# The first network's second and third row pieces by seven block products for eight

## What is computed

```python
def _swiglu(h, w_up, w_down):
    gate, up = jnp.split(h @ w_up, 2, axis=-1)
    return (jax.nn.silu(gate) * up) @ w_down

def _layer(x, W, st, is_prompt, page_table, mem):
    x = x + 0.5 * _swiglu(_rms_norm(x, g[0]), W['ffa_up'], W['ffa_down'])
    p = _rms_norm(x, g[1]) @ W['w_in']
    ...
    x = x + jnp.concatenate([o_rw, o_ml, o_nsa], axis=-1) @ W['w_out']
    x = x + _mem_attend(_rms_norm(x, g[2]), st['mem_kv'], W['mem_w_q'], W['mem_qk_g'][0], W['mem_w_o'])
    x = x + 0.5 * _swiglu(_rms_norm(x, g[4]), W['ffb_up'], W['ffb_down'])
```

## Time and profile before

| | |
|---|---|
| median of 3 runs | 3776.53 us (3775.8 to 3785.59) |
| the profiled execution | 3781.91 us, its span 3780.2 us, mean granted TensorE clock 0.941 |
| TensorE busy | 3462.8 us (92% of the span) |
| VectorE / ScalarE / GpSimd busy | 1558.4 / 640.7 / 304.4 us |
| chain of work that ended last | 82% TensorE, 9% VectorE, 3% transfers |
| second network's products (line 4420) | 879.0 us, 5544 instructions |
| first network's products (lines 411 and 421) | 682.4 us, 2112 instructions, and 332.8 us, 1056 instructions |

### The profile page before, as it was taken

The page is one execution under the profiler, slowest core; times in us unless marked ns, Lnnn a source line. Parts: engine busy times, 40 slices in busy tenths (PEclk is TensorE's granted clock), DMA queues, the critical chain, the costliest instruction groups (busy, mean ns, idle before and its releaser), DMA issues.

```text
span 3780.2 us, 51473 instructions
## 1 busy us (share of the span) xinstructions
PE 3462.8 (92%) x20460; PEld 2568.7 (68%) x20460; DVE 1558.4 (41%) x3874; ACT 640.7 (17%) x1525; POOL 304.4 (8%) x396
## 2 busy tenths in 40 slices
PE   6999898999999999997886968888888999999998
PEld 4666565666567777675664734444577998899998
DVE  3444603323322323313643458744364555344333
ACT  1000011001010101012223326550112111211111
POOL 3111100000000000001001100000012340000000
PEclk8999999999999999998687879999999999999999
DMA  6565554232334332334337413022035675456775
GB/s 159 172 184 175 174 155 108 87 98 76 88 115 117 101 102 75 95 120 112 48 79 165 131 54 122 7 74 83 15 120 179 209 229 188 130 166 208 233 235 184
DMA packets 630137, 488.74 MB, mean 129 GB/s; under 512 B 95068, under 2 KB 590028, under 8 KB 625420
## 3 DMA queue, kind: packets, MB, share of 16 engines
q1 hardware_dynamic: 601820, 400.62, 36.2%
q0 software_dynamic: 13824, 67.12, 5.8%
q10 hardware_dynamic: 14256, 17.71, 1.3%
HBM read 419.85 MB, written 70.73 MB: 130 GB/s over the span
## 4 chain that ended last, share of the span: by engine, by line
PE 82%; DVE 9%; DMA 3%; issue 2%; SPq 2%; ACT 2%; DVEq 0%; POOL 0%; ACTq 0%; POOLq 0%
PE psum L4420 21%; PE psum L411 17%; PE psum L421 9%; PE psum L442 7%; PE psum L451 4%; PE psum L3745 3%; PE psum L1387 2%; DVE arena L3602 1%; PE psum L3511 1%; PE psum L3521 1%; PE psum L2683 1%; PE psum L3903 1%; PE psum L3500 1%; PE psum L4018 1%; PE psum L2724 1%
## 5 line engine op out<-in xcount | busy, mean ns | idle before, releaser
L4420 PE MATMUL psum<-arena 128*128 128x192 f32 (+1 forms) x5544 | 879.0, 320 | 22.9 <-POOL arena L4413 10.1
L4420 PEld LDWEIGHTS psum<-arena 128*128 128x128 f32 x5544 | 863.5, 192 | 39.2 <-issue 12.7
L411 PE MATMUL psum<-arena 128*128 128x384 f32 (+1 forms) x2112 | 682.4, 478 | 21.8 <-DVE arena L559 11.8
L411 PEld LDWEIGHTS psum<-arena 128*128 128x128 f32 x2112 | 398.1, 193 | 250.2 <-issue 22.8
L421 PE MATMUL psum<-arena 128*128 128x384 f32 (+1 forms) x1056 | 332.8, 472 | 0.0
L421 PEld LDWEIGHTS psum<-arena 128*128 128x128 f32 x1056 | 197.3, 190 | 113.0 <-issue 0.7
L442 PE MATMUL psum<-arena 128*128 128x384 f32 (+3 forms) x816 | 268.2, 484 | 6.0 <-DVE arena L559 6.0
L442 PEld LDWEIGHTS psum<-arena 128*128 128x128 f32 (+1 forms) x816 | 151.5, 190 | 100.8 <-issue 22.2
L4558 DVE SCALAR_TENSOR_TENSOR arena<-psum,arena 128x192 f32<-128x192 f32 (+1 forms) x336 | 113.4, 345 | 197.5 <-PE psum L4420 195.8
L451 PE MATMUL psum<-arena 128*128 128x264 f32 (+3 forms) x576 | 135.6, 397 | 0.0
L3745 PE MATMUL psum<-arena 128*128 128x384 f32 (+1 forms) x384 | 123.9, 480 | 6.1 <-issue 6.1
...
...
## 6 DMA issues: line engine op xcount, KB each, us to landing
arena<-in_ffa_up SPq DMA_DIRECT2D x132, 512.0 KB, 5.3
arena<-in_ffb_up SPq DMA_DIRECT2D x88, 512.0 KB, 4.3
...
```

The source lines that it names most:

```text
L411: ins = mm(b[:, 0:n], w[:, g, k], hC[:, k, 0:n], start=(k == 0), stop=(k == KD - 1))
L4420: ins = pe.eng.matmul(out, left[:, k], right[:, k], start=(first and k == 0), stop=(k == n - 1), skip_group_check=True)
```

## The change

Pieces 1 and 2 of the first network are computed as the second network is. The code of the second network becomes a set of functions for any `Net`, `NET_A` being pieces 1 and 2 of the first and `NET_B` the three pieces of the second; piece 0 of the first stays as it was. For `NET_A` the weight sums are not stored: GpSimd and VectorE make them in both pieces. The ring `wring` holds gate weights (2 slots), lift weights (3) and one slot of sums, at the places where the projection's slabs lie, so that the first loads of a piece wait for the projection's last slabs (`begins`), and the first slabs for the network's last products. The dense step now comes before the lane step for TensorE, VectorE and ScalarE, and GpSimd weaves its sums with its lane steps. In both networks VectorE's steps are cut at other points: the last product's evacuation and the third weight sum now stand after the `yield`. The first product of a group no longer waits for the weight sums. The core of the diff (the `Net` versions of `load_lift` and so on replace those of the second network, which are otherwise the same):

```diff
-        wring = arena.take(P, 3, SLAB)
+        wring = arena.take(P, 5 * D + 3 * 512)
...
+        hT_all = arena.take(P, 3 * KD // 2 * (PIECE // 2))
+        act_all = arena.take(P, FH * PIECE)
+        actT = act_all.rearrange("p (f c) -> p f c", f=FH)
...
+        KEPT = FT + len(PASSES) * KD // 2
+        HW = PIECE // 2
+        gate_w, lift_w = wring[:, 0:2 * D].rearrange("p (s x) -> p s x", s=2), wring[:, 2 * D:5 * D].rearrange("p (s x) -> p s x", s=3)
+        sums_w = [wring[:, 5 * D:5 * D + 3 * 512], arena.array[:, consts_at:consts_end]]
+        hB, hT = hC, hT_all.rearrange("p (t k c) -> p t k c", t=3, k=KD // 2)
+        actB = actT[:, 0:6]
...
+        def begins(net, m):
+            return not net.joined and m % KEPT < 3
+
+        def load_lift(sp, net, m):
+
+            kind, c, q, x = net.groups[m]
+            s, _, n0 = loads_of(net, m)
+            if begins(net, m):
+                proj_used(sp, c - 1, 11 if s == 2 else 10)
+                if m >= KEPT + 2:
+                    sp.wait_ge(products_made, net.products[m - 3, "last"])
+            elif m >= 3:
+                sp.wait_ge(products_made, net.products[m - 3, "last"])
+            if 3 <= m < net.made + 3:
+                wait_third_stored(sp, net, m - 3)
+            sp.wait_ge(slab_in[s], n0)
+            w, src = left_of(net, m), weights_of(net, m, 1)
+            n = pairs_of(net, m)
+            dst = lift_w[:, m % 3, 0:2 * n * P].rearrange("p (k c) -> p k c", k=2 * n)
+            if m >= net.made:
+                src, dst = src[:, n:2 * n] if kind == "up" else src[:, 1:2 * n:2], w["A22"]
+            sp.eng.dma_start(dst, src, allow_slow_non_contiguous=True).then_inc(slab_in[s], 16)
+
+        def load_gate(sp, net, m):
+
+            c, s = net.groups[m][1], loads_of(net, m)[0]
+            if begins(net, m) and m % KEPT < 2:
+                proj_used(sp, c - 1, 9)
+            elif m >= 2:
+                sp.wait_ge(products_made, net.products[m - 2, "P2"])
+            if 2 <= m < net.made + 2:
+                sp.wait_ge(weights_summed, net.weights_0 + m - 1)
+                sp.wait_ge(evacuated, net.evacuations[m - 2, "S3"])
+            n = pairs_of(net, m)
+            sp.eng.dma_start(gate_w[:, m % 2, 0:2 * n * P].rearrange("p (k c) -> p k c", k=2 * n), weights_of(net, m, 0),
+                             allow_slow_non_contiguous=True).then_inc(slab_in[s], 16)
+
...
+        def load_group(sp, net, m):
+            load_lift(sp, net, m)
+            load_gate(sp, net, m)
+            if m >= net.made:
+                load_sums(sp, net, m)
...
+        def load_item(sp, n):
+
+            c, r = divmod(n, ITEMS)
+            if c == 3:
+                return
+            s, _, n0 = LOADED["in", c, r]
+            if r < KEPT and c:
+                load_group(sp, NET_A, KEPT * (c - 1) + r)
+                return
+            if r < KEPT:
...
+        def weight_sums_gp(gp, net, m):
+
+            w = left_of(net, m)
+            wait_group(gp, net, m)
+            if m >= 2:
+                gp.wait_ge(products_made, net.products[m - 2, "P3"])
+                wait_sums_stored(gp, net, m - 2)
+            gp.eng.tensor_tensor(w["S1"], w["A21"], w["A22"], ALU.add).then_inc(gpsimd_done, 1)
+            gp.wait_ge(gpsimd_done, gp.done(gpsimd_done))
+            gp.eng.tensor_tensor(w["S2"], w["S1"], w["A11"], ALU.subtract).then_inc(gpsimd_done, 1)
+            gp.wait_ge(gpsimd_done, gp.done(gpsimd_done))
+            gp.eng.tensor_tensor(w["S4"], w["A12"], w["S2"], ALU.subtract).then_inc(weights_summed, 1)
+            gp.wait_ge(weights_summed, net.weights_0 + m + 1)
+
+        def net_gp(gp, net, c):
+            if net.joined:
+                gp.wait_ge(out_v[2], 9 + NB + 2 * KD)
+            else:
+                proj_used(gp, c - 1, 11)
+            weight_sums_gp(gp, net, chunk_of(net, c)[0])
+            for m in chunk_of(net, c):
+                if (m + 1) % KEPT:
+                    weight_sums_gp(gp, net, m + 1)
+                yield
+                if net.groups[m][0] == "up":
...
+        def last_pe(pe, net, m):
+
+            kind, c, _, _ = net.groups[m]
+            pe.wait_ge(evacuated, net.evacuations[m, "u2" if kind == "up" else "P7"])
+            pe.wait_ge(summed, net.h_sums(c, 4) if kind == "up" else net.act_sums(m, 4))
+            product(pe, x_bank(net, m), left_of(net, m)["A22"], right_of(net, m)["T4"], first=False)
+
+        def net_pe(pe, net, c):
+            for m in chunk_of(net, c):
+                A, B = left_of(net, m), right_of(net, m)
+                up = net.groups[m][0] == "up"
+                x, y, z = x_bank(net, m), y_bank(net, m), z_bank(net, m)
+                if m == chunk_of(net, c)[0]:
+                    pe.wait_ge(h_made, pe.due(h_made, KD) - 4)
+                if m % KEPT or net.joined and m:
+                    pe.wait_ge(evacuated, net.evacuations[m - 1, "g2" if net.groups[m - 1][0] == "up" else "P3"])
+                wait_group(pe, net, m)
+                product(pe, x, A["A11"], B["B11"])
+                if m < net.made:
+                    pe.wait_ge(weights_summed, net.weights_0 + m + 1)
+                pe.wait_ge(summed, net.h_sums(c, 1) if up else net.act_sums(m, 1))
+                product(pe, z, A["S1"], B["T1"])
+                yield
+                if net.pends(m - 1):
+                    last_pe(pe, net, m - 1)
+                if up:
+                    pe.wait_ge(copies_made, net.copied(m, 0))
+                    pe.wait_ge(summed, net.h_sums(c, 2))
+                else:
+                    pe.wait_ge(evacuated, net.evacuations[m, "P1"])
+                    pe.wait_ge(summed, net.act_sums(m, 2))
+                product(pe, x, A["S2"], B["T2"], first=False)
+                if net.pends(m - 1):
+                    pe.wait_ge(evacuated, net.evacuations[m - 1, "last"])
+                product(pe, y, A["A12"], B["B21"])
+                if up:
+                    pe.wait_ge(copies_made, net.copied(m, 1))
+                else:
+                    pe.wait_ge(evacuated, net.evacuations[m, "P5"])
+                product(pe, z, A["S4"], B["B22"], first=False)
+                if up:
+                    yield
+                    pe.wait_ge(copies_made, net.copied(m, 2))
+                else:
+                    pe.wait_ge(evacuated, net.evacuations[m, "P6"])
+                if m < net.made:
+                    pe.wait_ge(evacuated, net.evacuations[m, "S3"])
+                pe.wait_ge(summed, net.h_sums(c, 3) if up else net.act_sums(m, 3))
+                product(pe, x, A["S3"], B["T3"], first=False)
+                if not net.pends(m):
+                    last_pe(pe, net, m)
...
+        def last_dve(v, net, m):
+
+            kind, c, q, x = net.groups[m]
+            h, X = half_of(c), x_bank(net, m)
+            v.wait_ge(products_made, net.products[m, "last"])
+            if kind == "down":
+                to_x(v, net, m, "last", 1, 0, X)
+                if not net.joined and q == len(PASSES) - 1:
+                    v.wait_ge(evacuated, net.evacuations[m, "last"])
+                    for k in (2 * x, 2 * x + 1):
...
+        def net_dve(v, net, c):
...
+                    to_x(v, net, m, "P1", 0, 0, x)
+                    to_x(v, net, m, "P5", 1, 1, z)
+                    yield
+                    last_dve(v, net, m - 1)
+                    third_sum_dve(v, net, m)
+                    to_x(v, net, m, "P6", 0, 1, x)
...
+                yield
+                if net.pends(m - 1):
+                    last_dve(v, net, m - 1)
+                third_sum_dve(v, net, m)
+                v.wait_ge(products_made, net.products[m, "P2"])
+                v.wait_ge(copies_made, net.copied(m, 0))
+                e.tensor_tensor(s1, y, s1, ALU.add).then_inc(evacuated, 1)
...
+                yield
+                v.wait_ge(products_made, net.products[m, "P7"])
+                e.tensor_tensor(s5, x, s5, ALU.add).then_inc(evacuated, 1)
...
+        def scale_and_sum_dve(v, net, gi, c):
+
+            c0, n = CH[c]
+            scale_begin_dve(v, n)
+            for half in range(2):
+                for k in range(4 * half, 4 * half + 4):
+                    scale_one_dve(v, gi, k, xT[:, k, c0:c0 + n], hB[:, k, 0:n], n)
+                v.wait_ge(h_made, v.counts[h_made.name])
+                first_h_sum_dve(v, net, c) if half == 0 else other_h_sums_dve(v, net, c)
...
+        def dense_dve(v, c):
+            ahead = c < 2
+            if c:
+                v.wait_ge(proj_full, A_A * c)
+                scale_and_sum_dve(v, NET_A, 0, c)
+            for _ in net_dve(v, NET_A, c) if c else plain_dve(v):
...
-                for _ in alternate(3, lane(gp, p, rw_begin_gp, rw_make_gp, rw_chain_gp), lane(gp, p, ml_begin_gp, ml_make_gp, ml_chain_gp)):
+                lanes = lane(gp, p, rw_begin_gp, rw_make_gp, rw_chain_gp), lane(gp, p, ml_begin_gp, ml_make_gp, ml_chain_gp)
+                if p == 0:
```

(3 more changed lines are left out.)

855 lines of the change are left out of this document (390 added, 465 removed).

## The result

The changed kernel takes 3829.7 us (median of four runs, 3822.9 to 3836.4) where the kernel before takes 3778.3 beside it: 1.0133 times the time, 95% interval 1.0109 to 1.0156. It is slower by some 50 us; the prediction was 3741, faster. The profiled execution has a span of 3821.0 us, 40.8 more than that of before.

A forecast was written before the change was run, and what follows sets the result against it. TensorE was taken to bound the kernel, nearly without gaps. 105.5 - 24 - 4 - 40 - 5 + 3 = 35.5 us off the profiled 3781.9 gave 3746, or 3741 against the median of 3776.5; range 3703 to 3789.

The forecast's parts named there:

- the price of the products: Pieces 1 and 2: 1848 half-width products each at 162.5 and 135.8 ns, 105.5 us less if nothing waits.
- the price of GpSimd's disturbance: Middle of both pieces: lane operations with two SBUF inputs grow by a quarter, raising 12 us a piece to 17 and 23.
- the clock: TensorE at 1.2 GHz behind two long starts and clusters of short waits: 5 us lost (0 to 15).
- starts, ends and middle waits: Pieces 1 and 2: 24 us later starts, 4 us for squares at the ends, 40 us of waits in the middle.
- the lane step of lines 1664 to 1683: A VectorE lane step that now follows a down group: 2.8 us of TensorE waiting.
- the second network: First product no longer waits for GpSimd, VectorE's steps stand beside products they read: 3 us gained (5 lost to 8 gained).
- the forecast: The main case, chance 0.52: the whole kernel faster, 3712 to 3765 us.
- the rival of a blocked VectorE: GpSimd's sums hold up every lane operation and VectorE in turn holds up P2: 3796 us, slower, chance 0.17.
- the two start waits: Sign of being right: TensorE waits before the lanes' first matmuls, some 17 us in piece 1, 7 in piece 2.
- Waits on GpSimd's third sum: Sign of being wrong: TensorE waiting for that weight sum in the middle of a piece; no size given.
- the cover that holds: Rival: lane steps start early enough, middle waits 12 us and starts 20, 3706 us in all; chance 0.20.
- late weights: Rival: gate loads land late, piece 2's 22 up groups wait 1 to 2 us each, 3774 us; chance 0.11.

The follow-up runs named there:

- Alone against alone: Old and new kernel with each piece's recurrent lanes run after the next piece's dense work instead of woven in: piece 1 353.2 us old form, 329.5 new.
- the thin sums: Changed kernel with GpSimd's first-network weight sums, from the third group on, made over 2 of every 128 columns: 3759.5 us, 0.9934 of the kernel before.

## Why the prediction was wrong

In the two pieces together the kernel before takes 855.6 us and the changed one 918.1: 62.5 more, where the terms of the sum gave 32.5 less. The steps that failed are the price of the products (105.5 us less, "if nothing waits"), the price of GpSimd's disturbance (16 of the 40 us for the middle) and the clock (5 us). The miss of 95 us splits into:

- **The products: 74.5 us.** Forecast 105.5 less, measured 656.8 - 625.8 = 31.0 less. Two errors stand in this one term. I took the old form's price from stretches full of lanes and the new form's from the second network, which has few; "the form thus costs what its columns cost" compared unlike neighbours. Alone against alone the saving is 65.4 us, so 40 of the 74.5 are this. The other 34 are what the lanes cost the new form more than the old, and that is the clock. At the full-clock prices of 169.6 and 143.7 ns the new products would take 579.0 us; I put the 46.8 above that down to 1.2 GHz, an estimate from two windows. The old ones lost some 5 us in this way: line 411 takes 336.5 and 283.5 ns in the two windows below, where the clock was 1.00, and 339.1 and 288.0 over the pieces. The breaks between short runs cost the new form no more than the old. **The clock term of 5 us** held the idea and not its size.
- **Idle time of TensorE: 17.8 us.** It grew by 85.8 (60.2 + 53.7 against 19.7 + 8.5) where starts, ends and middle waits made 68. The first 82 and 66 us hold 35.4 us more idle time than before, where I had 24: the long waits came, but the first product of piece 1 waited 7.9 us instead of 4.8 (5.1 in the kernel with the sums on VectorE, whose four scalings take 2.21 us instead of 5.05), and short waits of 1.3 to 2.3 us followed. The ends hold 2 us less than before, not 4 more. In the middle I counted 40 and find 24 and 28. With the thin sums it is 22.7 in both middles together, where I had counted 12 a piece without disturbance: that sum came out right, though not place by place, as the lane step of lines 1664 to 1683 shows; what GpSimd adds did not, 30 us of middle waits instead of 16.
- **Lanes and squares: 7.7 us** more busy time beside the products, of which the prediction had none; and the 5 us for the clock, counted already, go off.

Line 411 in the kernel before, at full clock:

```profile
780.00:900.00 120.00, 91.53 (x272) 50.45 (x272) 1.00 0.32 93
1400.00:1480.00 80.00, 62.38 (x220) 40.92 (x221) 1.00 0.35 94
```

Outside the pieces, the second network brought 22 instead of 3, a term for which the prediction had no count by groups; the projections behind piece 2 took 9.1 more, at a clock of 0.93 for 0.97, which no run takes apart.

**The wrong choice** was between the forecast and the rival of a blocked VectorE. Its mechanism was in the prediction with its row, but I counted 12 us a piece without it and took 17 and 23 with it, 16 us for the mechanism, by letting lane operations grow by a quarter. Measured, the two largest groups grow by 37 and 51% (348 to 478, 420 to 633 ns), a single-input one by 88%, and leaving the sums out gives 64.7 us in the two pieces. (The products run faster then, so this is another cut through the same 95 us and not to be added.) "GpSimd is idle 60% of the time" was the argument against it; GpSimd's 132 us in 485 sufficed. The rival's number, 3796, was too low as well: it carried the same 105.5.

Of what the prediction said would show it: the two start waits came, and no weight load was late in the middle of a piece. Waits on GpSimd's third sum in the middle, a sign of being wrong, came too, but only three, 3.6 us in piece 1 and 2.2 in piece 2. A clock of 0.95, product lines at 162 and 136 ns and piece 1 under 450 us did not come, and the stretch behind 1780 changed by more than 8 us. The rivals of the cover that holds and of late weights are both out.

The thin sums show the rest of the truth: even without GpSimd's sums the two pieces take 853.4 us against 855.6 before. Their products take 605.1 us, 51.7 less than the old ones, and TensorE's idle time takes 48.0 back: 26.8 at the starts, where loads and lane steps come later, and 22.7 in the middle, where the old form's runs of 5.3 us hid the lane steps; the ends give 1.5. GpSimd's lock comes on top. That the lanes make most of the loss is shown by the two kernels with the lanes moved away; how it splits between breaks, waits and clock is worked out from rows, not tried.
